# A two-layer trunk on one core: products of the output projection moved between the steps of the first attention's last head

## The chip, the core and the metric

The kernel runs on one core of one Trainium2 chip. The metric is the time of one execution on the device in microseconds. Before the change it is 2202.14 us, the median of 3 runs (2201.82 to 2206.84).

TensorE multiplies, VectorE, ScalarE and GpSimd work on tiles, SyncE issues the transfers. Each engine takes its instructions in order; semaphores order them between engines. SBUF is the on-chip memory, PSUM holds what TensorE writes.

## The reference

Sequence 1024, width 1024, two layers. The part that matters here is the first attention and its output projection:

```python
q = rms_norm(q, q_g) * (A_HEAD_DIM ** -0.5)      # 8 heads, 2 maps of 64 each
k = rms_norm(k, k_g)
...
logits = jnp.einsum('bqhcd,bkhcd->bhcqk', q_blk, k)
logits = logits - slopes * dist                  # chunk-causal mask
p = jax.nn.softmax(logits, axis=-1)
wts = p[:, :, 0] - lam * p[:, :, 1]
return jnp.einsum('bhqk,bkhe->bqhe', wts, v)     # per block of 128 queries
...
o = rms_norm(o, subln_g) * (1.0 - lambda_init)
return o.reshape(b, s, A_HEADS * A_V_DIM) @ w_o  # added to x
```

Behind it come a squared-ReLU MLP, shared keys and values, a second attention with a sliding window, and a second MLP.

## The kernel before, in words

Every operand of a matmul is a pair of a high part (a copy rounded by ScalarE) and a low part (the subtraction value minus high part), and a product is three matmuls: high x high, high x low, low x high. "High products" are the two that read the high part of the activations.

The attention works head by head; one head has eight steps, one for each block of 128 queries. In step s TensorE makes the scores of block s, VectorE adds the distances and takes the maxima (custom operation, L1730 or, in the last head, L1770) and their negation (`nm_a`), ScalarE the exponentials, and VectorE mixes the two maps: a reciprocal, a factor (`coef_a`, L1744) and the mixing itself (L1749, reads `p` and `p1`, writes `p`). TensorE transposes the mixed weights (L2233), ScalarE and VectorE make their high and low part (`wT_hi`, `wT_lo`), and TensorE multiplies them with the values into `pv`. In heads 0 to 6 the same steps carry the projection of the next head's queries, keys and values (`proj<-wa`), which fills TensorE. The last head (`last_head`) has none of it. Its order is written out by hand: ahead of the loop scores 0 and 1 and block 7 of head 6, then for s = 0 to 6 the transposes of block s, the scores of block s+2 and the values of block s.

Head outputs are normalised by GpSimd (`norm_steps` and one multiplication of 128x1024; for the last head VectorE does it), transposed and stored as chunk c of `oT`. ScalarE's `high_early(c)` copies chunk c into `a_hi`; VectorE subtracts it into `a_lo`.

The output projection has 8 panels of 128 output columns. A panel is 8 chunks x 2 halves of the sequence x 3 matmuls of 512 columns, 384 in all. Its weights come by DMA into `w_raw` (two buffers in `w_quad`) and are split into `w_hi`, `w_lo` (three slots in `w_op`, so panel 3 needs panel 0's slot). Before the change panels 0 and 1 are split in the last head. Behind the head's last values products TensorE makes the high products of chunks 0 to 6 for panels 0 and 1 (56), then the low ones (28), then in `segment` chunk 7 of both and all of panel 2, 3 and so on. `add_x(i)` on VectorE adds the residual stream (loaded into `quad`) to panel i and frees its bank; ScalarE then scales and squares it, and only then copies the high part of panel i+3 or, at i = 0, panel 3.

Of the kernel before, what the change touches and what calls it, by code (L numbers as in the profile page):

```python
# [32 lines left out]
ALU = mybir.AluOpType  # L33
ACT = mybir.ActivationFunctionType
F32 = mybir.dt.float32
# [4 lines left out]
P = 128  # L40
# [28 lines left out]
EARLY_LOW = 3  # L69
WB_AT = {1: (0, 1), 2: (1, 3), 3: (3, 4), 4: (4, 6), 5: (6, KC)}  # L70
# [96 lines left out]
def trunk(nc, io):  # L167
    ctx = ExitStack()
    with ctx:
# [58 lines left out]
        scope = ExitStack()  # L228
        x_tok = [sb("x_tok0", [P, 4, D], F32, scope)]
# [85 lines left out]
        w_quad = [sb(f"w_quad{i}", [P, 2, 4, 256], F32) for i in range(2)]  # L315
        w_op = sb("w_op", [P, 7, 2, HALF], F32R)
# [10 lines left out]
        def panel_parts(seg, i):  # L327

            return w_first if seg and i == 0 else (w_hi[i % 3], w_lo[i % 3])

# [20 lines left out]
        small_mm, sinks_done, lam_exp = sem("small_mm"), sem("sinks_done"), sem("lam_exp")  # L351
# [44 lines left out]
        out_tr, out_staged = sem("out_tr"), sem("out_staged")  # L396
        vs_in = sem("vs_in")


        dve_passed, act_passed = sem("dve_passed"), sem("act_passed")  # L400
# [194 lines left out]
        def _(sp):  # L595
# [49 lines left out]
            w_out = (io["a_w_o"][0], io["b_w_o"][0])  # L645
            w_up, w_down = io["mlp_w_up"], io["mlp_w_down"]

            def segment(seg):
# [3 lines left out]
                def load_wo(i):  # L652
                    if i >= 2 or seg:
                        sp.wait_ge(w_lo_done, KC * seg + i - 1)
                    sp.dma_start(w_raw[i % 2], wo[:, :, P * i:P * (i + 1)]).then_inc(w_in[i % 2], 16)
# [25 lines left out]
                load_wo(2)  # L681
                if seg == 0:
                    load_wo(3)
# [143 lines left out]
        def _(pool):  # L827
# [56 lines left out]
            run_heads(pool, head)  # L884

            def segment(seg):
# [12 lines left out]
                if seg == 0:  # L899
                    pool.wait_ge(tr_ready, 144)  # L900
                else:
                    pool.wait_ge(ot_free, 32)
                clear()
                def sum_weights(n, part):
# [130 lines left out]
        def _(act):  # L1035
# [23 lines left out]
            def first_head():  # L1059
# [19 lines left out]
                act.wait_ge(sinks_done, 1)  # L1079
# [4 lines left out]
                act.wait_ge(small_mm, 1)  # L1084
                nc.scalar.activation(lam_e[:, :], score[0][:, 0:2], ACT.Exp).then_inc(lam_exp, 1)
# [5 lines left out]
            def split_panel(panel):  # L1091
                i = panel % KC
                act.wait_ge(w_in[i % 2], panel // 2 * 16 + 16)
# [16 lines left out]
            def exps(h, s, par, i):  # L1110
                keys = P * (s + 1)
                act.wait_ge(nm_ready, h * NB + s + 1)
                act.sem_inc(act_passed, 1)
# [22 lines left out]
            def last_head():  # L1136
# [4 lines left out]
                def last_exps(s):  # L1141
                    keys, i = P * (s + 1), s % 2
                    act.sem_inc(act_passed, 1)
# [5 lines left out]

# [1612 lines left out]
```

## Time and profile before

| What | Value |
|---|---|
| median of the runs | 2202.14 us |
| profiled execution: span from first to last instruction | 2202.5 us |
| TensorE matmuls busy | 2147.4 us, 97% |
| VectorE | 1569.2 us, 71% |
| ScalarE | 1137.3 us, 52% |
| GpSimd | 758.0 us, 34% |
| mean granted clock of TensorE | 0.991 |

The page gives no time of the profiled execution beside its span. A line of a timeline is: start in us, duration in us, engine, line of the kernel, operation, output<-inputs, shape, count, and in brackets the idle time before it and what ended it. PE is TensorE, DVE VectorE, ACT ScalarE, POOL GpSimd. In merged lines (x7) the duration is that from the first start to the last end. Matmul ends are modelled, so the distance of two starts tells the rate. The granted clock is the share of 2.4 GHz that TensorE had; 0.5 is its lower level of 1.2 GHz.

### The profile page before, as it was taken

The page shows a single profiled execution, that of the slowest core. Times are in us where ns is not written, and L with a number is a line of the kernel's source. Part 1 is how long each engine was busy: PE and PEld are TensorE (multiplying, and loading weights), DVE is VectorE, ACT ScalarE, POOL GpSimd, SP SyncE. Part 2 cuts the span into 40 slices and gives each one's busy share as a digit, 9 for nine tenths or more (in the row PEclk, how much of TensorE's full clock was granted, in tenths as well). Part 3 has the DMA queues.
Part 4 walks back from the last instruction along what each step waited for, and adds up shares of the span by engine and source line. Part 5 has one row for each costly group of instructions (what it writes and reads, how often), then busy time and mean ns, then how long its engine had stood idle before and what let it go on. Part 6 is the DMA issues. An engine that isn't in the chain of part 4 may idle for free.

```text
span 2202.5 us, 34714 instructions
## 1 busy us (share of the span) xinstructions
PE 2147.4 (97%) x11580; PEld 1844.2 (84%) x11580; DVE 1569.2 (71%) x3012; ACT 1137.3 (52%) x2429; POOL 758.0 (34%) x1199
## 2 busy tenths in 40 slices
PE   7999999988999999999999999999999999999999
PEld 6999999977878888787888899988888888788787
DVE  6788788877586666778767757774766666886783
ACT  5566666655554555624434446764455555443342
POOL 2334333331642222333235225434622222322331
PEclk9999999999999999999999999999999999999999
DMA  6111110002424444754534121105244445754352
GB/s 201 47 30 30 29 29 22 1 20 96 131 99 158 157 146 142 273 178 171 191 124 160 63 55 48 29 19 164 91 158 156 141 141 212 259 191 144 104 183 85
DMA packets 190916, 257.71 MB, mean 117 GB/s; under 512 B 15136, under 2 KB 139552, under 8 KB 186144
## 3 DMA queue, kind: packets, MB, share of 16 engines
q1 hardware_dynamic: 190752, 255.65, 35.0%
q8 instruction: 87, 1.43, 0.3%
q14 instruction: 77, 0.63, 0.1%
HBM read 174.09 MB, written 79.69 MB: 115 GB/s over the span
## 4 chain that ended last, share of the span: by engine, by line
PE 80%; DVE 11%; issue 5%; ACT 2%; DMA 1%; POOLq 1%; DVEq 0%; POOL 0%; ACTq 0%; SPq 0%
PE score L2190 41%; PE proj L2190 15%; PE trb L2190 14%; PE pv L2190 6%; DVE xop L1543 4%; DVE w_op L1543 2%; DVE xT L1863 1%; PE trb L2233 1%; ACT p L1115 1%; DMA xop<-u_dram 1%; PE trb L2601 0%; PE trb L2287 0%; DVE p L1730 0%; PE trb L2261 0%; PE score L2588 0%
## 5 line engine op out<-in xcount | busy, mean ns | idle before, releaser
L2190 PE MATMUL score<-xop,w_op 128*128 128x512 f32 x3840 | 891.5, 391 | 7.2 <-DVE xT L1863 5.5
L2190 PEld LDWEIGHTS score<-xop,w_op 128*128 128x128 f32 x3840 | 722.3, 189 | 161.3 <-issue 11.0
L2190 PE MATMUL trb<-xop,w_op 128*128 128x512 f32 x1536 | 362.1, 391 | 5.4 <-DVE xT L1863 4.7
L897 POOL TENSOR_TENSOR w_quad<-w_quad,w_sum 128x512 f32<-128x512 f32 x64 | 83.8, 1309 | 777.0 <-DVE w_op L1543 777.0
L2190 PEld LDWEIGHTS trb<-xop,w_op 128*128 128x128 f32 x1536 | 287.3, 188 | 69.1 <-DVE w_op L1543 7.5
L1037 ACT ACTIVATE w_op<-w_quad 128x512 fp32r<-128x512 f32 (+1 forms) x336 | 213.9, 643 | 229.7 <-PE score L2190 106.6
L1543 DVE TENSOR_TENSOR w_op<-w_quad,w_op 128x512 fp32r<-128x512 f32 (+1 forms) x336 | 297.3, 890 | 40.8 <-ACT w_op L1037 40.7
L1863 DVE TENSOR_TENSOR xT<-score,xT 128x512 f32<-128x512 f32 x160 | 109.2, 686 | 138.0 <-PE score L2190 132.0
L1543 DVE TENSOR_TENSOR xop<-xop 128x1024 fp32r<-128x1024 f32 x112 | 150.6, 1361 | 3.5 <-ACT xop L1037 3.5
L1037 ACT ACTIVATE quad<-score 128x512 f32<-128x512 f32 x96 | 57.2, 596 | 176.0 <-PE score L2190 174.8
L1037 ACT ACTIVATE xop<-xop 128x1024 fp32r<-128x1024 f32 x112 | 117.0, 1053 | 56.5 <-DMA xop<-u_dram 56.2
L2190 PE MATMUL proj<-wa_hi,a_hi 128*128 128x384 f32 x418 | 142.5, 341 | 0.8 <-DVE v_parts L1544 0.8
L1115 ACT ACTIVATE p<-p,nm_a,slopes 128x128 f32<-128x128 f32 (+7 forms) x112 | 96.4, 862 | 90.4 <-DVE nm_a L1735 90.4
L2190 PE MATMUL proj<-wa_hi,a_lo 128*128 128x384 f32 x418 | 139.9, 335 | 0.0
L2190 PE MATMUL proj<-wa_lo,a_hi 128*128 128x384 f32 x418 | 139.8, 334 | 0.0
L1863 DVE TENSOR_TENSOR quad<-trb,quad 128x512 f32<-128x512 f32 x64 | 44.2, 690 | 106.0 <-PE trb L2190 72.2
L1037 ACT ACTIVATE w_op<-w_sum 128x512 fp32r<-128x512 f32 x128 | 76.9, 625 | 81.8 <-PE trb L2190 32.8
L2190 PE MATMUL score<-a_hi,w_op 128*128 128x512 f32 x368 | 112.8, 392 | 0.0
L519 POOL TENSOR_TENSOR chain_p<-rstd_qk 128x8 f32<-128x8 f32 x96 | 19.3, 201 | 248.8 <-DVE rstd_qk L511 239.5
L911 POOL TENSOR_TENSOR w_sum<-w_quad 128x512 f32<-128x512 f32 x64 | 90.0, 1407 | 36.2 <-DMA w_quad<-in_mlp_w_down 25.7
L897 POOL TENSOR_TENSOR w_quad<-w_quad 128x512 f32<-128x512 f32 x64 | 99.8, 1560 | 5.0
L1730 DVE CUSTOM_DVE_ANT_0 p<-score,dist_a 128x128 f32<-128x128 f32 (+7 forms) x112 | 80.3, 754 | 29.7 <-PE score L2190 29.7
(319 smaller groups left out, 4293.9 us busy)
## 6 DMA issues: line engine op xcount, KB each, us to landing
xop<-u_dram SPq DMA_DIRECT2D x112, 512.0 KB, 5.1
u_dram<-quad SPq DMA_DIRECT2D x32, 1536.0 KB, 9.7
w_quad<-in_mlp_w_up SPq DMA_DIRECT2D x64, 512.0 KB, 5.6
w_quad<-in_mlp_w_down SPq DMA_DIRECT2D x64, 512.0 KB, 4.9
wa_raw<-in_a_w_qkv SPq DMA_DIRECT2D x96, 128.0 KB, 2.4
quad<-xT_dram SPq DMA_DIRECT2D x32, 256.0 KB, 3.7
xT_dram<-xs SPq DMA_DIRECT2D x32, 256.0 KB, 2.4
u_dram<-quad SPq DMA_DIRECT2D x32, 256.0 KB, 3.8
```

Of the source, the lines that this page charges most:

```text
L519: eng.tensor_tensor(t, out, out, ALU.mult)
L897: return pool.tensor_tensor(out, x, y, ALU.subtract)
L911: pool.tensor_tensor(w_full(n, "S1"), quarter(n, 1, 0), quarter(n, 1, 1), ALU.add)\
L1037: return nc.scalar.activation(out, in_, ACT.Copy, scale=scale)
L1115: nc.scalar.activation(p[:, 0:keys], p[:, 0:keys], ACT.Exp, bias=nm_a[i][:, c:c + 1], scale=one(slopes, h), accum_out=ssum[par][:, c, s:s ...
L1543: return nc.vector.tensor_tensor(out, full, hi.bitcast(F32), ALU.subtract)
L1730: nc.vector.tensor_tensor_reduce(out=p[:, 0:keys], in0=score[c][:, 0:keys], in1=dist_a[:, S - keys:S], scale=1.0, scalar=LOWEST, op0=ALU.a ...
L1863: return nc.vector.tensor_tensor(out, a, b, ALU.add)
L2190: return nc.tensor.matmul(out, a, b, start=start, stop=stop, **kw)
L2233: last = nc.tensor.transpose(trb[b][:, P * (kc - 4 * i):P * (kc - 4 * i + 1)], p0[block_s % 2][:, P * kc:P * (kc + 1)], ident[:, :])
```

## The change

- Panel 2 is loaded into a place of its own and split in head 6 (step 2), first of all panels. Panel 0's high part is made at the beginning of the last head, panel 1's in its step 2; both low parts are GpSimd's.
- ScalarE makes the high parts of chunks 0 to 5 at the beginning of the last head; their low parts are GpSimd's, one behind the other, behind panel 1's.
- TensorE makes high products of chunks 0 to 5 of panel 2 between the steps of the last head, in the bank `proj`: first those of the right half (12). ScalarE copies the result into `kept`, and GpSimd adds it to the residual stream later, in `quad`. Then 12 of the left half. 12 more, of panel 1, stand ahead of the last values products.
- Behind the head stand the rest of chunks 0 to 5 for three panels, then chunk 6, then chunk 7; panel 2 is no longer a full panel in `segment`.
- Some semaphores are merged (`passed`, `lam_steps`), without a new wait.

```diff
+LATE = 6
+SPLIT_ORDER = (2, 0, 1, 3, 4, 5, 6, 7)
...
@@ sync: loads
+            sp.wait_ge(wa_lo_done, NH * 4)
+            sp.dma_start(w_raw2, w_out[0].rearrange("(k p) n -> p k n", p=P)[:, :, 2 * P:3 * P])\
+                .then_inc(w_in[0], 16)
...
@@ gpsimd
+                    if isinstance(h, int) and h == NH - 2 and s == NB - 1:
+                        low_panel()
...
+            def low_panel():
+
+                pool.wait_ge(w_lo_done, split_count(0, 2))
+                pool.wait_ge(w_hi_done, split_count(0, 0))
+                pool.tensor_tensor(w_lo[0], w_raw[0], w_hi[0].bitcast(F32), ALU.subtract).then_inc(w_lo_done, 1)
+
+            def last_head():
+
+                pool.wait_ge(o_rstd, NH - 1)
+                norm_steps(rstd_o[:, :], chain_o, NB)
...
+                pool.wait_ge(w_hi_done, split_count(0, 1))
+                pool.tensor_tensor(w_lo[1], w_raw[1], w_hi[1].bitcast(F32), ALU.subtract).then_inc(w_lo_done, 1)
+                for c in range(LATE):
+                    pool.wait_ge(o_early_hi, c + 1)
+                    pool.tensor_tensor(a_lo[:, c, :], oT[:, c, :], a_hi[:, c, :].bitcast(F32), ALU.subtract)\
+                        .then_inc(o_split, 1)
...
+                    x = quad[1][:, TILE[0, 1], :]
+                    pool.tensor_tensor(x, x, kept[0][:, :], ALU.add).then_inc(half_added, 1)
...
@@ scalar, last_head
+                high_early(0)
+                high_early(1)
                 last_exps(0)
                 high_wT(uses, 0)
+                split_panel(0)
+                high_early(2)
+                high_early(3)
...
                     if s == 1:
-                        high_early(0)
+                        high_early(4)
+                        high_early(5)
                     if s == 2:
+                        keep(0)
+                        split_panel(1)
                         high_pair(uses, h, 1, par)
...
-                    if s >= 4:
-                        high_early(s - 3)
...
-                    if s >= 5:
-                        split_panel(s - 5)
...
@@ vector
-                    if s == NB - 1:
-                        split_panel(0)
                     mix(h, s, par, s % 2)
...
-                split_panel(1)
...
-            for c in range(EARLY[0]):
+            dve.wait_ge(o_split, LATE)
+            for c in range(LATE, EARLY[0]):
...
@@ tensor
+            def panel_high(out, panel, half, chunks):
+
+                for c in chunks:
+                    pe.wait_ge(o_early_hi, c + 1)
+                    x_h = a_hi[:, c, HALF * half:HALF * (half + 1)]
+                    mm(out, w_hi[panel][:, c, :], x_h, c == 0, False)
+                    last = mm(out, w_lo[panel][:, c, :], x_h, False, c == LATE - 1 and (panel, half) == (2, 1))
+                return last
...
-                    for k in range(EARLY[seg] if i < 2 - seg else 0, KC):
+                    for k in range(EARLY[seg] if i < 3 - 2 * seg else 0, KC):
```

TensorE in the last head, step 5: transposes (`trb<-ident,p`), scores, values (`pv`). Before:

```order
L2233 MATMUL trb<-ident,p_1 128x128 [waits tr_free1]
L2233 MATMUL trb<-ident,p_1 128x128
L2190 MATMUL score<-kT_hi,qT_hi 128x512 [waits score_max]
...
L2190 MATMUL score<-kT_hi,qT_lo 128x512 x2
L2190 MATMUL pv<-v_parts,wT_hi 128x256 [waits tr_free1,tr_free0]
...
L2233 MATMUL trb<-ident,p_0 128x128 [waits tr_free0,mixed]
```

And after:

```order
L2247 MATMUL score<-kT_hi,qT_lo 128x512 x2
L2247 MATMUL proj<-a_hi,w_op 128x512 [waits o_early_hi]
L2247 MATMUL proj<-a_hi,w_op 128x512
...
L2247 MATMUL proj<-a_hi,w_op 128x512 [waits o_early_hi]
L2247 MATMUL proj<-a_hi,w_op 128x512
L2247 MATMUL pv<-v_parts,wT_hi 128x256 [waits tr_free1,tr_free0]
...
L2290 MATMUL trb<-ident,p_0 128x128 [waits tr_free0,mixed]
```

Six products of panel 2 now stand between the scores of block 7 and the values of block 5, ahead of the transposes of block 6.

GpSimd from the normalisation of head 6's output on. Before:

```order
L527 TENSOR_TENSOR rstd_o<-rstd_o,chain_p 128x8
L880 TENSOR_TENSOR xT<-xT,rstd_o 128x1024
L889 MEMSET ss 128x512 [waits tr_ready]
L889 MEMSET ss 128x512
L897 TENSOR_TENSOR quad<-quad 128x512 [waits h_ready]
```

And after:

```order
L542 TENSOR_TENSOR rstd_o<-rstd_o,chain_p 128x8
L915 TENSOR_TENSOR xT<-xT,rstd_o 128x1024
L918 TENSOR_TENSOR w_op<-w_quad,w_op 128x1024 [waits w_hi_done]
L921 TENSOR_TENSOR a_lo<-xT,a_hi 128x1024 [waits o_early_hi] x6
L929 MEMSET ss 128x512 [waits tr_ready,half_kept]
L929 MEMSET ss 128x512
L948 TENSOR_TENSOR quad<-quad,kept 128x512 [waits quad_in1]
L937 TENSOR_TENSOR quad<-quad 128x512 [waits h_ready]
```

Seven subtractions of 128x1024 stand where GpSimd had nothing until the end of the head.

TensorE in `segment`, from chunk 7 of panel 2 (`proj` and `pv`) to panel 3 (`score`). After the change:

```order
L2247 MATMUL proj<-a_hi,w_op 128x512 [waits o_split,w_lo_done]
L2247 MATMUL proj<-a_lo,w_op 128x512
L2247 MATMUL proj<-a_hi,w_op 128x512
L2247 MATMUL pv<-a_hi,w_op 128x512
L2247 MATMUL pv<-a_lo,w_op 128x512
L2247 MATMUL pv<-a_hi,w_op 128x512
L2247 MATMUL score<-a_hi,w_op 128x512 [waits o_split,xs_ready,w_lo_done]
```

Panel 2 has 6 products left there; before it had all its 48 between panel 1 and panel 3.

## Rows read from the trace of the kernel before

**Rows 1.** Windows: length, PE, PEld, DVE, ACT, POOL busy us (count), clock, DMA

```profile
460.00:480.00 20.00, 17.57 (x124) 16.01 (x123) 15.76 (x46) 10.47 (x24) 5.33 (x19) 0.97 0.20 53
480.00:500.00 20.00, 15.10 (x89) 11.47 (x90) 16.71 (x53) 13.45 (x37) 8.24 (x24) 0.78 0.01 1
500.00:520.00 20.00, 13.85 (x85) 11.81 (x82) 17.20 (x33) 17.39 (x37) 0.00 (x0) 0.82 0.18 51
620.00:640.00 20.00, 18.70 (x84) 14.22 (x84) 18.56 (x27) 9.26 (x18) 12.03 (x9) 1.00 0.21 65
640.00:660.00 20.00, 20.00 (x90) 16.53 (x89) 13.70 (x22) 11.30 (x21) 6.35 (x5) 1.00 0.43 146
```

**Rows 2.** Waits of TensorE, 470 to 700 us

```profile
PE pv L2190 <- DVE wT_lo L1543: 7.1, 4, 2.2
PE score L2190 <- DVE mx_a L1770: 4.1, 4, 1.5
PE trb L2233 <- DVE p L1749: 1.3, 2, 0.9
```

**Rows 3.** Timeline of VectorE, mixings of steps 4, 5 and 6

```profile
496.57 0.89 DVE L1749 SCALAR_TENSOR_TENSOR p<-p,coef_a,p 128x640 f32<-128x640 f32 x1
...
501.76 1.02 DVE L1749 SCALAR_TENSOR_TENSOR p<-p_last,coef_a,p 128x768 f32<-128x768 f32 x1
...
507.19 1.15 DVE L1749 SCALAR_TENSOR_TENSOR p<-p,coef_a,p 128x896 f32<-128x896 f32 x1
```

**Rows 4.** Timeline of TensorE in the last head

```profile
477.63 0.36 PE L2190 MATMUL pv<-v_parts,wT_hi 128*128 128x256 f32 x1 [2.14 <-DVE wT_lo L1543]
...
509.78 0.93 PE L2233 MATMUL trb<-ident,p 128*128 128x128 f32 x7
...
519.40 0.37 PE L2190 MATMUL pv<-v_parts,wT_hi 128*128 128x256 f32 x1 [2.22 <-DVE wT_lo L1543]
...
522.77 9.41 PE L2190 MATMUL score<-a_hi,w_op 128*128 128x512 f32 x40
```

**Rows 5.** Timeline of TensorE, first products of panels 2 and 3

```profile
545.59 0.39 PE L2190 MATMUL proj<-a_hi,w_op 128*128 128x512 f32 x1
...
556.47 0.39 PE L2190 MATMUL score<-a_hi,w_op 128*128 128x512 f32 x1
```

**Rows 6.** Timelines of ScalarE and VectorE: weights' copy; splits of panels 3 and 5

```profile
475.59 1.06 ACT L1037 ACTIVATE wT_hi<-trb 128x512 fp32r<-128x512 f32 x2
...
546.83 1.04 ACT L1037 ACTIVATE w_op<-w_quad 128x1024 fp32r<-128x1024 f32 x1
...
547.91 1.69 DVE L1543 TENSOR_TENSOR w_op<-w_quad,w_op 128x1024 fp32r<-128x1024 f32 x1 [2.78 <-ACT w_op L1037]
...
567.61 1.21 DVE L1543 TENSOR_TENSOR w_op<-w_quad,w_op 128x1024 fp32r<-128x1024 f32 x1
```

**Rows 7.** Timelines of VectorE and GpSimd in earlier heads

```profile
129.89 0.22 DVE L1744 SCALAR_TENSOR_TENSOR coef_a<-ssum,neg_lam,rcp_a 128x1 f32<-128x1 f32 x1
...
134.00 1.08 DVE L1744 SCALAR_TENSOR_TENSOR coef_a<-ssum,neg_lam,rcp_a 128x1 f32<-128x1 f32 x1
134.02 1.05 POOL L873 TENSOR_TENSOR qk<-qk,rstd_qk 128x512 f32<-128x512 f32 x1
...
385.38 1.90 POOL L880 TENSOR_TENSOR xT<-xT,rstd_o 128x1024 f32<-128x1024 f32 x1
...
385.53 1.77 DVE L1735 TENSOR_SCALAR nm_a<-mx_a,slopes 128x2 f32<-128x2 f32 x1
```

**Rows 8.** Timelines of GpSimd and VectorE, last head and behind it

```profile
490.92 2.34 POOL L880 TENSOR_TENSOR xT<-xT,rstd_o 128x1024 f32<-128x1024 f32 x1
...
491.42 0.82 DVE L1770 CUSTOM_DVE_ANT_0 p<-score,dist_a 128x640 f32<-128x640 f32 x1
...
599.29 1.30 POOL L897 TENSOR_TENSOR w_quad<-w_quad 128x512 f32<-128x512 f32 x1
...
614.52 1.28 DVE L1543 TENSOR_TENSOR xop<-quad,xop 128x512 fp32r<-128x512 f32 x2
...
619.74 3.46 DVE L1543 TENSOR_TENSOR xop<-quad,xop 128x512 fp32r<-128x512 f32 x2
```

More of the change, by code:

```diff
@@ L228, in trunk @@
         scope = ExitStack()
+        kept = [sb(f"kept{i}", [P, HALF], F32, scope) for i in range(1)]
+        scope.close()
+        scope = ExitStack()
         x_tok = [sb("x_tok0", [P, 4, D], F32, scope)]
@@ L329, in panel_parts, with split_count @@
             return w_first if seg and i == 0 else (w_hi[i % 3], w_lo[i % 3])
+        def split_count(seg, panel):
+            return KC * seg + (panel if seg else SPLIT_ORDER.index(panel)) + 1
         oT = xT
@@ L680, in segment @@
                 load_wo(1)
-                load_wo(2)
-                if seg == 0:
-                    load_wo(3)
+                load_wo(2 if seg else 3)
                 sp.wait_ge(o_split, KC * seg + 5)
@@ L1092, in split_panel @@
                 i = panel % KC
-                act.wait_ge(w_in[i % 2], panel // 2 * 16 + 16)
+                act.wait_ge(w_in[i % 2], panel // 2 * 16 + (16 if panel else 32))
                 if i >= 3 or panel == KC + 2:
@@ L1225, in head @@
                         wa_split(h + 2, par == 0, 0, 1)
+                    if s == 2 and isinstance(h, int) and h == NH - 2:
+                        act.wait_ge(w_in[0], 16)
+                        copy(w_hi[2], w_raw2).then_inc(w_hi_done, 1)
                     if s == O_STEP and tail:
@@ L1699, in head @@
                         low_pair(uses, h, s, par)
+                    if s == 2 and isinstance(h, int) and h == NH - 2:
+                        dve.wait_ge(w_hi_done, split_count(0, 2))
+                        low(w_lo[2], w_raw2, w_hi[2]).then_inc(w_lo_done, 1)
                     if s in (2 if attn else 4, NB - 1) and more:
@@ L1882, in add_x @@
                         dve.wait_ge(quad_in[u % 2], 64 * (2 * seg + u // 2 + 1))
+                        if seg == 0 and (i, half) == (2, 1):
+                            dve.wait_ge(half_added, 1)
                         if i:
@@ L2362, in head, with panel_low @@
                         values(uses, s, (s - 1) % NB, h * 4 + (s - 1) // 2, par if s else 1 - par)
+            def panel_high(out, panel, half, chunks):
[5 more added lines that the diff above has]
+                return last
+            def panel_low(out, panel, half, chunks, first):
+                for c in chunks:
+                    pe.wait_ge(o_split, c + 1)
+                    mm(out, w_hi[panel][:, c, :], a_lo[:, c, HALF * half:HALF * (half + 1)], first and c == 0, False)
             def panel_products(seg, panel, x_hi, x_lo, k):
@@ L2396, in _ @@
             transpose_weights(last_uses, 0, NB - 1, NH * NB - 1)
+            pe.wait_ge(score_max, 2 * NH * NB)
+            pe.wait_ge(w_lo_done, split_count(0, 1))
+            panel_high(wo_bank[0][1][0], 1, 0, range(LATE))
             values(last_uses, 0, NB - 1, NH * 4 - 1, 1)
[L2400 to L2415 removed]
+            panel_high(wo_bank[0][1][1], 1, 1, range(LATE))
+            for half in range(2):
+                panel_high(wo_bank[0][0][half], 0, half, range(LATE))
+            transpose_outputs(last_uses, NH, 1)
+            for half in range(2):
+                panel_low(wo_bank[0][0][half], 0, half, range(LATE), False)
+            for half in range(2):
+                panel_low(wo_bank[0][1][half], 1, half, range(LATE), False)
+            pe.wait_ge(pv_free, NH * 4)
+            for half in range(2):
+                panel_low(wo_bank[0][2][half], 2, half, range(LATE), half == 1)
+            for panel in range(3):
+                for half in range(2):
+                    panel_high(wo_bank[0][panel][half], panel, half, range(LATE, EARLY[0]))
+            for panel in range(3):
+                for half in range(2):
+                    panel_low(wo_bank[0][panel][half], panel, half, range(LATE, EARLY[0]), False)
             def segment(seg):
                 for i in range(KC):
[L2419 removed]
+                    pe.wait_ge(w_lo_done, split_count(seg, i))
                     if i >= 3:
```

97 lines of the change are left out of this document (56 added, 41 removed).

## The prediction

> **What bounds the kernel now.** I read the windows of 20 us first [rows 1]. TensorE is busy in all of a window after the first attention (640 to 660 us: 20.00 of 20), but only 17.57, 15.10 and 13.85 us in the three windows from 460 to 520 us. That is the last head of the first attention, which ends at 522.77 us [rows 4]. In two of them the granted clock is 0.78 and 0.82. So everywhere else TensorE sets the time, and here something else does. The list of waits [rows 2] names it: 7.1 us for the low parts of the transposed weights, 4.1 us for the maxima, 1.3 us for the mixed weights, all by VectorE. VectorE's own line in that head is serial: mixing of step s, two maxima of step s+1, two exponentials on ScalarE, mixing of step s+1. The mixings start at 496.57, 501.76 and 507.19 us [rows 3], 5.2 and 5.4 us apart, and VectorE has 17.20 us of work in 20 [rows 1]. A delay of one mixing therefore moves the end of the head by nearly as much; work given to TensorE's gaps does not, as long as it fits.
>
> The clock shows in the matmuls. The sixteen values products of the last block, 256 columns each, stand between 519.40 and 522.77, behind a gap of 2.22 us: 0.211 us each, which is the 1.2 GHz level [rows 4]. From 522.77 on TensorE runs without a gap and at full clock: 48 products of 512 columns lie from 545.59 to 556.47, 0.227 us each [rows 5].
>
> **What the change removes.** The output panels have the same 384 products. Before, all of them stand behind 522.77. Now 24 lie between the head's steps and 12 ahead of the last values products, so 348 remain: 36 x 0.227 = 8.2 us less behind the last head. That is the whole direct gain. The gaps that ought to take the 36 are there: rows 2 sum to 12.5 us, with 2.14 us where four of them go and 2.22 us where twelve go. VectorE also loses the low parts of two panels in the head and of six chunks and a panel behind it, but none is on the line: the first ran beside the last exponentials, and TensorE did not wait for any of those behind. ScalarE has less to do at the very end, worth at most the 1.0 us of one such copy. The early split of panel 2 in head 6 (one ScalarE copy of 1.04 us, one VectorE subtraction of 1.2 us, both [rows 6]) lies in a stretch in which TensorE is full and VectorE is not: nothing, with 1.2 us as the price if it is not covered.
>
> **What it adds: GpSimd beside VectorE.** Eight subtractions of 128x1024 go to GpSimd: the low part of panel 0 at the beginning of the head, that of panel 1 and of six chunks in its second half. The trace before has none of this size. One of 128x512 with two tensors takes 1.30 us and the next starts behind it; the normalisation of 128x1024 takes 1.90 us [rows 7, 8]. I take 2.4 us each, from 1.9 to 2.6.
>
> Rows 7 show what such an operation does to VectorE. The negated maxima took 1.77 us, started 0.15 us into a GpSimd operation of 1.90 us and until its end; the mixing's factor, 0.22 us elsewhere, took 1.08 us against a GpSimd operation of 1.05 us. Where GpSimd has one operation behind the other, it takes the turn after each of VectorE's: two subtractions with two SBUF tensors take 1.28 us alone and 3.46 us beside it, 1.73 each [rows 8]. The maxima, which read PSUM and one SBUF tensor, are not hit: 0.82 us in the middle of GpSimd's normalisation, 491.42 against 490.92 [rows 8]. Of the chain, the factor and the mixing have two tensors in SBUF. The Trainium skill ("SBUF — State Buffer", section "SBUF: two separate sides") has a rule that speaks against this change: the port pair of VectorE and GpSimd is an exclusive lock, and the loser blocks for the whole instruction. By that rule each collision costs the rest of a GpSimd operation; were bandwidth merely shared, a mixing of 1 us could lose about 1 us. The trace agrees with the lock.
>
> Now the line, step by step. *Step 0.* ScalarE finishes the copies of the last weights of head 6 at 476.65 [rows 6], then panel 0's high part, 477.6. GpSimd's first subtraction runs from 477.7 to 480.1; the factor of mixing 0, ready at 478.7, waits: +1.5 to 2.1 us, of which waits that were there before take some. I keep +1.3 us. *Step 4.* GpSimd's normalisation ended at 493.26 before (490.92 + 2.34, rows 8), now about 494.5. Panel 1: to 497.0. Chunk 0: to 499.4. The factor, due 0.3 us ahead of mixing 4 and 1.3 to 1.9 us later than before (497.6 to 498.2), waits to 499.4; chunk 1 takes the turn between factor and mixing, to 502.0. Mixing 4 starts at 502.0, not 496.57: +5.4. *Step 5.* Due 5.2 us later. Chunks 2 and 3 run 502.9 to 507.7, the factor follows, chunk 4 goes ahead of the mixing: 510.3, not 501.76: +8.5. *Step 6.* Chunk 5 is over at 513.7 and the factor is due at 515: no wait, +8.1. Bounds for this item: 2 mixings x 2.4 = 4.8 us if all the factors fall free, 9.5 if none does; and, if VectorE were served first each time, 2 us.
>
> *Steps 6 and 7 on TensorE.* Six products now stand between the last scores and the values of block 5, ahead of the transposes of block 6, which start at 509.78 [rows 4], 1.4 us behind the mixing's end, and which ScalarE's last exponentials follow. At full clock they cost 1.4, at half 2.6 us. Delayed as above TensorE has long gaps, so I expect much of it at the lower level: +1.6, from 0 to 3.1. *The end.* Twelve products, 2.7 to 5.1 us, go into a gap of 2.2: +1 to 2; against that the last values products may get the full clock (3.4 us down to half of it) and ScalarE is free earlier: +0.4, from -1.5 to +1.5. The head ends 8.1 + 1.6 + 0.4 = 10.1 us later.
>
> **What it adds behind.** Before, panel 2's 48 products (545.59 to 556.47) covered the preparation of panel 3, whose slot is free only when panel 0 is complete: ScalarE's copy at 546.83 to 547.87, VectorE's subtraction at 547.91 to 549.60 [rows 6]. Panel 0 completes at 544.2 in that time. Now panels 1 and 2 have 12 products left after it, 2.7 us, so TensorE is there at 546.9 and waits until 549.6: 2.7 us. No other engine gets sooner there; ScalarE has the scaled and squared chunk 0 in front. The gap of 2.22 us in rows 4 was followed by 3.4 us at the lower level, which cost half of that: I take 1.3, from 0 to 1.7. From panel 4 on VectorE is ready in time, at its times of before: panel 5's subtraction ends at 568.8 [rows 6], and TensorE, at 549.6 + 1.3 + 2 x 10.9, asks for it at 572.7. The 1.3 us TensorE lacks at 620 to 640 [rows 1] is a wait that moves with panel 7. The copy of the half panel (0.6 us, ScalarE) and its addition (1.3 us, GpSimd) lie in idle time, as the early loads do.
>
> **Sum.** -8.2 + 10.1 + 2.7 + 1.3 = +5.9 us on the profiled span of 2202.5 us, which is 0.4 above the median of 2202.14. The page gives no other time for that execution. Forecast: 2202.1 + 5.9 = 2208.0 us; the case's own range is 2203 to 2213.
>
> **Rivals.** (A) *The gaps win.* VectorE is hit once a step or less, the head ends only 2 us later or not at all. For it: no mixing in the trace was ever longer than its shape asks, even with GpSimd starting right behind. Against it: the factor in front always took the wait, and GpSimd had nothing more queued. -8.2 + 2 + 4 = -2.2 us, 2200; without the 2 us and with the last values products at full clock, -6, 2196. If panel 3's low part were ready as well, -10: the case spans 2192 to 2202. The Trainium skill ("TensorE: Matmul & The Clock Gate", part 1) says that activity releases the clock; by it, filled gaps would speed up the last values products and more in the head; the rows show only that gaps above 2 us came before the lower level. (B) *The clock falls with the longer head.* Place: steps 5 to 7. With 9 us steps TensorE is idle nearly half of each, and scores, six products and values all run at 1.2 GHz: +3.1 in place of 1.6, twelve products 5.1, values 3.4, chain +9.5. Sum +10: 2212 us. It decides from the point at which GpSimd's operations cost more than about 8 us. (C) *The 24 products are not hidden.* TensorE was late for the transposes of block 6 even before (1.4 us, above); then the head only grows by what is moved into it, with GpSimd harmless: -8.2 + 8 + 4 = +4, 2206 us.
>
> **Chances.** Forecast 0.52, A 0.24, B 0.14, C 0.10. About 0.3% (6.6 us: 2195.5 and 2208.7) is what a measurement of this kernel tells from no change. Slower by more: under half of the forecast's case (0.23), most of B (0.13), a little of C (0.02): 0.38. Faster by more: under half of A, 0.10. Within: 0.52. Range 2196 to 2213: it holds the forecast's case, C, the lower half of B and over half of A.
>
> **What would show it.** In the profile after: mixings of 640 and 768 elements starting 2 us or more behind their factor; a factor of 1 us and more; mixing 6 near 515; the last values products ending near 532; a wait of 2.7 us of TensorE for a low part, with all panels behind complete. If the mixings keep a distance of 5.2 us, the second term is wrong and A holds. If TensorE runs through from panel 2 to 3, the third is.

## The result, and the profile after

| | median | ratio to the kernel before |
|---|---|---|
| kernel before | 2202.86 us (17 runs) | |
| kernel after | 2209.04 us (17 runs) | 1.0024, interval 1.0018 to 1.0030 |

The change makes the kernel 0.24% slower, some 5.3 us, with 36 products taken out from behind the last head. The forecast was 2208.0 us. The profiled execution after has a span of 2207.7 us, clock 0.992.

To compare traces I measure from a common point, the start of the mixing of 128x1024 in head 6: 471.80 us before, 473.20 after. In the fourteen traces of this study it lies between 468.2 and 473.2, and the changed kernel itself has it at 473.20 and, in run 5, at 472.28. Of the 1.4 us between the two, 1.1 us are there at TensorE's first product already (8.1 and 9.2 us); 0.1 us is head 6, in which the change splits panel 2. Each row is one trace. Distances to the starts of the named operations, in us ("MLP" is the one behind the first attention):

| | mixing 4 | 5 | 6 | 7 | last values product | first MLP product | end of span |
|---|---|---|---|---|---|---|---|
| before | 24.8 | 30.0 | 35.4 | 42.6 | 50.8 | 139.1 | 1730.7 |
| after | 27.5 | 35.0 | 42.5 | 49.6 | 56.4 | 140.6 | 1734.5 |

Windows of 20 us, columns as in rows 1 with GB/s at the end, after:

```profile
480.00:500.00 20.00, 14.55 (x93) 11.41 (x93) 16.59 (x54) 14.32 (x35) 14.93 (x31) 0.91 0.03 7
500.00:520.00 20.00, 14.39 (x81) 11.24 (x79) 18.74 (x32) 9.70 (x25) 13.50 (x6) 0.83 0.23 73
520.00:540.00 20.00, 17.80 (x101) 15.38 (x101) 9.64 (x25) 6.99 (x18) 0.89 (x2) 1.00 0.00 1
540.00:560.00 20.00, 17.67 (x74) 14.27 (x73) 5.28 (x6) 6.16 (x9) 6.09 (x5) 0.95 0.55 176
...
600.00:620.00 20.00, 19.14 (x84) 15.21 (x82) 13.75 (x14) 10.08 (x18) 16.43 (x12) 1.00 0.30 97
```

GpSimd is busy for 14.93 and 13.50 us where it had 8.24 and 0.00 [rows 1]. TensorE lacks 2.3 us at 540 to 560 and 0.9 at 600 to 620, where it was busy for 20.00 of 20 before:

```profile
540.00:560.00 20.00, 20.00 (x90) 16.57 (x89) 7.80 (x8) 9.62 (x16) 11.73 (x8) 1.00 0.75 242
...
600.00:620.00 20.00, 20.00 (x89) 16.44 (x88) 15.74 (x18) 14.27 (x27) 13.10 (x10) 1.00 0.32 106
```

VectorE's factors and mixings of steps 4 to 6, and beside them GpSimd, after:

```profile
499.59 1.01 DVE L1801 SCALAR_TENSOR_TENSOR coef_a<-ssum,neg_lam,rcp_a 128x1 f32<-128x1 f32 x1
500.68 2.89 DVE L1806 SCALAR_TENSOR_TENSOR p<-p,coef_a,p 128x640 f32<-128x640 f32 x1
...
507.83 0.34 DVE L1801 SCALAR_TENSOR_TENSOR coef_a<-ssum,neg_lam,rcp_a 128x1 f32<-128x1 f32 x1
508.24 3.04 DVE L1806 SCALAR_TENSOR_TENSOR p<-p_last,coef_a,p 128x768 f32<-128x768 f32 x1
...
515.69 1.15 DVE L1806 SCALAR_TENSOR_TENSOR p<-p,coef_a,p 128x896 f32<-128x896 f32 x1
```

```profile
495.88 2.38 POOL L918 TENSOR_TENSOR w_op<-w_quad,w_op 128x1024 fp32r<-128x1024 f32 x1
498.21 15.29 POOL L921 TENSOR_TENSOR a_lo<-xT,a_hi 128x1024 fp32r<-128x1024 f32 x6
```

Mixing 4 takes 2.89 us for 0.89 of work, mixing 5 3.04 for 1.02 [rows 3]. Each lost 2.0 us inside its own row, so the wait stands in the duration and not as a distance from the factor. GpSimd waits in the same way: of the six subtractions in the merged row, four take 2.34 to 2.40 us, and the two during which a mixing had its turn take 2.94 and 3.10. The third mixing, behind GpSimd's end at 513.5, has its old 1.15 us. TensorE at the head's end, at panel 3 and at the MLP's operands, after:

```profile
525.00 3.01 PE L2247 MATMUL score<-a_hi,w_op 128*128 128x512 f32 x12
527.85 0.28 PE L2247 MATMUL pv<-v_parts,wT_hi 128*128 128x256 f32 x1
...
557.66 0.50 PE L2247 MATMUL score<-a_hi,w_op 128*128 128x512 f32 x1 [2.33 <-DVE w_op L1597]
...
613.80 2.61 PE L2247 MATMUL score<-xop,w_op 128*128 128x512 f32 x9
617.15 0.96 PE L2247 MATMUL score<-xop,w_op 128*128 128x512 f32 x3 [0.74 <-DVE xop L1597]
```

Sixteen values products now lie between 527.85 and 529.76: 0.12 us each, the upper clock level, against 0.211 in rows 4. The wait of 2.33 us at panel 3 is new. So is one of 0.74 us for an operand of the MLP.

### The profile page after: what moved, and what is told of

It reads as the page before. It is cut to its first block, busy times and chain, and to the rows that moved or that the text cites. A ratio compares the mean times of both kernels' runs of the same rounds, so it can differ in the third digit from the quotient of the medians.

```text
span 2207.7 us, 34721 instructions
## 1 busy us (share of the span) xinstructions
PE 2146.4 (97%) x11580; PEld 1840.8 (83%) x11580; DVE 1571.0 (71%) x3004; ACT 1138.0 (52%) x2430; POOL 781.1 (35%) x1208
## 4 chain that ended last, share of the span: by engine, by line
PE 76%; DVE 12%; issue 6%; ACT 2%; POOL 2%; DMA 1%; POOLq 1%; DVEq 0%; SPq 0%; ACTq 0%
PE score L2247 39%; PE proj L2247 15%; PE trb L2247 13%; PE pv L2247 6%; DVE xop L1597 4%; DVE w_op L1597 2%; DVE xT L1918 1%; PE trb L2290 1%; ACT p L1161 1%; POOL quad L937 1%; DMA xop<-u_dram 1%; POOL ss L934 1%; PE trb L2693 1%; PE trb L2344 0%; DVE p L1787 0%
## 5 line engine op out<-in xcount | busy, mean ns | idle before, releaser
L1787 DVE CUSTOM_DVE_ANT_0 p<-score,dist_a 128x128 f32<-128x128 f32 (+7 forms) x112 | 80.3, 754 | 27.2 <-PE score L2247 27.1
```

Source lines behind the costliest of these rows:

```text
L1787: nc.vector.tensor_tensor_reduce(out=p[:, 0:keys], in0=score[c][:, 0:keys], in1=dist_a[:, S - keys:S], scale=1.0, scalar=LOWEST, op0=ALU.a ...
```

## The experiments

Twelve runs in three groups (1 to 4, 5 to 8, 9 to 12), each group against the kernel before on the same chip (medians 2201.83, 2201.95 and 2201.66 us, so times of different groups are compared by their ratios). The intervals are 0.09 to 0.14% wide to each side, 2 to 3 us; a smaller difference between two runs is read from the traces, one for each run, or stays open. Distances as above:

| | ratio (interval) | mixing 4 | 5 | 6 | 7 | last values | first MLP | end |
|---|---|---|---|---|---|---|---|---|
| 1 chunks' low parts to VectorE | 1.0019 (1.0009 to 1.0028) | 25.6 | 30.9 | 36.4 | 43.5 | 50.3 | 137.6 | 1730.9 |
| 2 before + GpSimd work | 1.0038 (1.0024 to 1.0052) | 27.2 | 35.2 | 41.4 | 48.6 | 55.0 | 143.1 | 1734.8 |
| 3 GpSimd behind the mixings | 0.9988 (0.9979 to 0.9997) | 23.5 | 28.9 | 34.3 | 41.4 | 48.2 | 130.7 | 1726.9 |
| 4 panel 3 first | 1.0021 (1.0011 to 1.0030) | 28.5 | 36.1 | 43.6 | 50.6 | 57.5 | 137.5 | 1733.2 |
| 5 changed, again | 1.0021 (1.0010 to 1.0031) | 27.5 | 35.0 | 42.5 | 49.6 | 56.4 | 140.7 | 1734.6 |
| 6 panel 0 first | 1.0007 (0.9999 to 1.0016) | 27.5 | 35.0 | 42.5 | 49.6 | 56.4 | 136.3 | 1730.4 |
| 7 runs 3 and 6 | 0.9974 (0.9965 to 0.9983) | 24.8 | 29.9 | 35.4 | 42.5 | 49.3 | 129.2 | 1723.3 |
| 8 twelve behind | 1.0034 (1.0021 to 1.0047) | 27.5 | 35.0 | 42.5 | 49.7 | 56.6 | 143.6 | 1735.9 |
| 9 run 6, addition later | 1.0009 (1.0000 to 1.0018) | 28.5 | 36.1 | 43.5 | 50.6 | 57.4 | 137.4 | 1728.8 |
| 10 run 7, addition later | 0.9972 (0.9961 to 0.9982) | 24.8 | 30.0 | 35.4 | 42.5 | 49.3 | 129.3 | 1722.6 |
| 11 run 10, load later | 0.9966 (0.9954 to 0.9979) | 23.5 | 28.8 | 34.3 | 41.4 | 48.2 | 128.2 | 1720.8 |
| 12 values first | 1.0042 (1.0028 to 1.0056) | 28.2 | 35.7 | 43.2 | 51.8 | 59.3 | 147.9 | 1740.9 |

### GpSimd beside the mixings: runs 1, 2 and 3

Run 1 takes GpSimd's chunks away:

```diff
-                for c in range(LATE):
-                    pool.wait_ge(o_early_hi, c + 1)
-                    pool.tensor_tensor(a_lo[:, c, :], ...).then_inc(o_split, 1)
...
-            dve.wait_ge(o_split, LATE)
-            for c in range(LATE, EARLY[0]):
+            for c in range(EARLY[0]):
```

> The changed kernel with the six low parts of the activations given back to VectorE, behind the last head; the two low parts of weights stay with GpSimd. Theory (GpSimd's long two-input operations block the factor and then the mixing): only panel 1's subtraction is left beside the mixings, so mixing 4 starts near 498.6 instead of 500.7, mixing 5 near 503.8 instead of 508.2, mixing 6 near 509 instead of 515.7; the last values products end about 6 us earlier (523 to 524). Behind the head VectorE makes seven low parts at 1.15 us each and is late for TensorE by 1 to 3 us. Median 2203.5 to 2207 against 2209.0 of the changed kernel. Rival (the six products between steps and the longer TensorE path set the head's length, GpSimd is harmless): the head ends where it did, 529 to 530, and the time is 2210 or more.

The mixings are back within 1.0 us of before, and the head ends 6.1 us earlier than after the change (50.3 against 56.4), with all 36 products where the change put them. TensorE waited three times 0.63 us for VectorE's chunks, 1.9 us in all. Little of it reaches the end: 2205.54 us, by the ratio 1 us under the changed kernel, which the intervals don't separate, and 3.6 us by the trace. The chunks cost 1.9 us of waits, and the granted clock behind these was 0.57 and 0.58 from 536 to 540 us, an estimated 1.7 us more. Waits of 2.5 us at panel 3 and 2.2 us at the MLP's operands followed. So a head of the old length alone doesn't make this kernel faster than the kernel before: the low parts that GpSimd had made in the head are missed behind it.

Run 2 adds GpSimd's work alone to the kernel before:

```diff
+            def last_head():
+                head(NH - 1, 1, True, True, False, False)
+                ...
+                for c in range(7):
+                    last = pool.tensor_tensor(a_lo[:, c, :], w_raw[1], w_raw[1], ALU.subtract)
```

> The kernel before with one addition: GpSimd makes seven more subtractions of 128x1024 behind its normalisation in the last head, into a place that is free there (their result is overwritten unread). Nothing else is changed, TensorE's work least of all. Theory (lock, and GpSimd takes the turn between factor and mixing): mixing 4 starts near 500.5 instead of 496.57, mixing 5 near 508.5 instead of 501.76, mixing 6 near 514 instead of 507.19; the last values products end 6 to 7.5 us later; median 2208.5 to 2210.5 against 2202.9. Rival one (a lock, but VectorE is served next): only the factor waits, 1 to 2 us in all, head 2 to 3.5 us longer, 2205 to 2206.5. Rival two (shared bandwidth or no contention; the lengthening in the changed kernel comes from TensorE's products): less than 1.5 us, 2203 to 2204.5.

2209.16 us, 0.38% slower. Without a single product moved, this is at least as slow as the changed kernel. The profiled execution was the fastest of the five, 2204.79 us; its trace shows 4.1 us of the 8 (1734.8 against 1730.7), and where the rest arises in the slower executions it can't show. One line was added on VectorE too, a wait for the last subtraction ahead of the split of panel 1; that subtraction ends at 503.3 us, well ahead of it. VectorE and GpSimd there:

```profile
493.49 1.86 DVE L1752 SCALAR_TENSOR_TENSOR coef_a<-ssum,neg_lam,rcp_a 128x1 f32<-128x1 f32 x1
495.42 2.44 DVE L1757 SCALAR_TENSOR_TENSOR p<-p,coef_a,p 128x640 f32<-128x640 f32 x1
501.72 1.62 DVE L1752 SCALAR_TENSOR_TENSOR coef_a<-ssum,neg_lam,rcp_a 128x1 f32<-128x1 f32 x1
503.41 1.02 DVE L1757 SCALAR_TENSOR_TENSOR p<-p_last,coef_a,p 128x768 f32<-128x768 f32 x1
```

```profile
489.74 13.58 POOL L889 TENSOR_TENSOR a_lo<-w_quad 128x1024 fp32r<-128x1024 f32 x7
```

A factor of one column took 1.86 and 1.62 us instead of 0.22, and the mixing behind the first took 2.44 instead of 0.89: GpSimd took the turn between the two. Taken singly, its third subtraction ends at 495.33, where the factor ends (495.35), and its fourth runs from 495.30 to 497.18, inside the mixing. Mixings 4, 5 and 6 came 2.4, 5.2 and 6.0 us later, where 3.9, 6.7 and 6.8 were expected; these subtractions, whose two operands are one tile, took 1.89 us each when undisturbed, not 2.4. Rival two falls. Rival one too, by the second row: had VectorE been served next, that mixing would have kept its 0.89 us.

Run 3 leaves GpSimd five of the eight subtractions and releases each by a mixing's end (`ON_POOL` is 3; VectorE makes the other chunks behind the head):

```diff
+                pool.wait_ge(mixed, (NH - 1) * NB + 4)
+                low_panel()
+                pool.wait_ge(mixed, (NH - 1) * NB + 5)
                 pool.wait_ge(w_hi_done, split_count(0, 1))
...
-                for c in range(LATE):
+                for c in range(ON_POOL):
+                    pool.wait_ge(mixed, (NH - 1) * NB + 6 + min(c, 1))
```

> The changed kernel with GpSimd's subtractions each released by the end of a mixing: panel 0 behind mixing 3, panel 1 behind mixing 4, chunk 0 behind mixing 5, chunks 1 and 2 behind mixing 6; chunks 3 to 6 by VectorE behind the head. Theory (lock): each subtraction of 2.4 us fits between a mixing and the next factor (some 4 us), so mixings 4, 5 and 6 start within 0.7 us of their times before the change (496.6, 501.8, 507.2); the last values products end at 523 to 524.5 instead of 529.8; median 2202 to 2204.5 against 2209.0. Rival (sharing: what GpSimd does costs VectorE the same wherever it stands): the head still ends 4 us or more later than before the change, 2206 or more.

2197.53 us, 0.12% faster than before the change and by the ratios 8 us under the changed kernel. The five subtractions that stay in GpSimd lengthen none of VectorE's factors and mixings when they stand behind a mixing:

```profile
498.43 2.38 POOL L924 TENSOR_TENSOR a_lo<-xT,a_hi 128x1024 fp32r<-128x1024 f32 x1 [3.11 <-DVE p L1809]
504.00 4.73 POOL L924 TENSOR_TENSOR a_lo<-xT,a_hi 128x1024 fp32r<-128x1024 f32 x2 [3.19 <-DVE p L1809]
```

```profile
497.34 1.02 DVE L1809 SCALAR_TENSOR_TENSOR p<-p_last,coef_a,p 128x768 f32<-128x768 f32 x1
502.47 0.22 DVE L1804 SCALAR_TENSOR_TENSOR coef_a<-ssum,neg_lam,rcp_a 128x1 f32<-128x1 f32 x1
502.76 1.15 DVE L1809 SCALAR_TENSOR_TENSOR p<-p,coef_a,p 128x896 f32<-128x896 f32 x1
```

Between the mixings at 497.34 and 502.76 VectorE's maxima read PSUM; GpSimd's 2.38 us fit beside them, and the factor keeps 0.22 us. The head ends 2.6 us earlier than before the change, with the 36 products in it: 520.0 on the scale of the trace before, 3 us better than the 523 to 524.5 expected. I had counted the products at the end as a cost. Some 1.1 us of the 2.6 go with the clock of this one execution: it was 1.00 all through the head, while runs 7 and 10, with the same head and 0.88 to 0.95 from 480 to 500 us, have mixing 4 at 24.8 and the end at 49.3. The time too is below what was expected: by the ratio 2200.2 us on the scale of 2202.86, against 2202 to 2204.5. The Trainium skill ("SBUF — State Buffer", section "SBUF: two separate sides") calls the port pair of the two engines an exclusive lock; by that rule the waits of runs 2 and 3 come out as they did, and both traces agree.

### TensorE's products in the head: runs 5, 8 and 12

Run 5 is the changed kernel again. Run 8 takes twelve products of steps 4 to 6 back behind the head. Run 12 does so with the twelve of panel 1:

```diff
-                    if s == 4: ... panel_high(proj[:, :], 2, 0, (0,))
-                    if s == 5: ... (1, 2, 3)
-                    if s == 6: ... (4, 5)
...
             panel_high(wo_bank[0][1][1], 1, 1, range(LATE))
+            pe.wait_ge(half_kept, 1)
+            panel_high(proj[:, :], 2, 0, range(LATE))
```

```diff
-            panel_high(wo_bank[0][1][0], 1, 0, range(LATE))
             values(last_uses, 0, NB - 1, NH * 4 - 1, 1)
+            panel_high(wo_bank[0][1][0], 1, 0, range(LATE))
```

> The changed kernel once more, unaltered, to stand beside the other runs of this chip: 1.0024 times the kernel before, that is 5 to 6 us above it.

> The changed kernel with the twelve products of panel 2's left half taken out of steps 4, 5 and 6 of the last head and put behind its last values products; the rest as changed. Prediction's term (six products in steps 6 and 7 lengthen the head by 1.6 us): the head ends 1.6 us earlier, 12 x 0.227 = 2.7 us come behind it, median 1.1 us above the changed kernel. Theory now, from the trace (with mixings held up by GpSimd the twelve products lie wholly in TensorE's gaps): the head ends where it did, median 2.2 to 3 us above the changed kernel. Rival (the head's own length follows TensorE's work): no more than the changed kernel.

> The changed kernel with the twelve products of panel 1 moved from ahead of the last values products to behind them. Prediction's term (twelve products against the clock of the values, in all +0.4 us for the head): the head ends 0.4 us earlier, 2.7 us more behind it, +2.3 us. Theory from the trace (the twelve keep TensorE busy so that the sixteen values products run at 0.12 us each and not 0.21, and they fill what is otherwise a wait): without them TensorE waits about 2.2 us for the low part of the weights, the values take 3.4 us, and the head ends at the same time or up to 0.6 us later; the time is 2.5 to 3.5 us above the changed kernel. Rival (the values run at full clock anyway): the head ends 1 us earlier or more, the time is 1.7 us above or less.

Run 8: the last values product at 56.6 against 56.4, the first MLP product 2.9 us later, the median 2.3 us above run 5, as expected (the intervals overlap; the 2.9 us of the trace carry the reading). The twelve had been hidden; the head's length does not follow them. Run 12: the values of the last block and what is ahead of them:

```profile
512.69 0.64 PE L2247 MATMUL score<-kT_hi,qT_lo 64*128 64x512 f32 x2
513.26 2.10 PE L2247 MATMUL proj<-a_hi,w_op 128*128 128x512 f32 x6
...
516.62 0.93 PE L2290 MATMUL trb<-ident,p 128*128 128x128 f32 x7
...
525.34 0.55 PE L2247 MATMUL pv<-v_parts,wT_hi 128*128 128x256 f32 x1 [1.67 <-DVE wT_lo L1597]
525.69 0.41 PE L2247 MATMUL pv<-v_parts,wT_lo 128*128 128x256 f32 x1
525.90 0.41 PE L2247 MATMUL pv<-v_parts,wT_hi 128*128 128x256 f32 x1
```

The values go at 0.21 us each (525.69 to 525.90), the lower level, behind a gap of 1.67 us. From mixing 7 to the last values product it is 7.4 us; 6.8 with the twelve in front. The time is about 4 us above the changed kernel by the ratios, more than the 2.5 to 3.5 expected, and the head ends 2.9 us later (59.3 against 56.4), where 0.6 at most was expected. In the trace 2.2 of the 2.9 us lie ahead of mixing 7, on which this edit has no hold: in this execution the scores of block 7 (510.57 to 513.3) also ran at the lower level, and the transposes of block 6 began at 516.62, 2.9 us behind their mixing's end (1.4 us after the change), so mixing 7 came 8.6 us behind mixing 6. It is 7.1 in the traces of runs 4, 5, 6 and 9. This is the prediction's term for steps 6 and 7, at its price, in one execution of the six that carry those products beside GpSimd's chunks.

### Behind the head: runs 4, 6, 7, 9, 10 and 11

Run 4 moves ScalarE's copy of panel 3 ahead of the scaled chunk 0:

```diff
                 for i in range(KC - 1):
+                    if i == 0 and not seg:
+                        split_panel(3)
-                    if i + 2 < KC and (seg or i):
+                    if i + 2 < KC and (seg or i > 1):
                         split_panel(KC * seg + i + 2)
```

> The changed kernel with one line's order changed on ScalarE: the copy of panel 3's high part stands ahead of the scaled and squared chunk 0, not behind. Theory (panel 3's low part is late because its preparation starts only when panel 0 is complete, and the wait of 2.3 us brings the lower clock): the copy runs about 2.4 us earlier, TensorE waits 0.5 us or less at panel 3, no product behind it is at the lower level, and what is behind comes 3 to 4 us earlier: median 2205 to 2206.5 against 2209.0. Rival (the wait only moves: the chunk 0 work that is now later delays the residual panel 3 or GpSimd's sums, and the MLP starts as late): 2207.5 to 2209.

The wait at panel 3 is gone. By the ratio the time is that of run 5, 1.0021. Waits of TensorE from 596 to 660 us (total, times, longest):

```profile
PE score L2249 <- DVE xop L1599: 3.4, 2, 2.6
PE proj L2249 <- DVE ss L1978: 0.3, 1, 0.3
```

What TensorE gained at panel 3 it waited for at the MLP's first operands, 3.4 us, with the clock from 600 to 620 us at 0.91. The wait moved, as the rival had it; something else is due there. Whether all of the time went with it stays open: from the last values product to the end the trace has 2.3 us less than the changed kernel, and the ratios don't resolve that.

Run 6 changes only the order of TensorE's products, so that panel 0 is complete first and the others' products stand behind it:

```diff
             transpose_outputs(last_uses, NH, 1)
-            ... low products, chunk 6 and its low part, panel by panel
...
+                    if seg == 0 and i < 3:
+                        ... the same for panel i, just ahead of its chunk 7
                     for k in range(EARLY[seg] if i < 3 - 2 * seg else 0, KC):
```

> The changed kernel with TensorE's order behind the last head altered: after the high products and the transposes panel 0 is brought to its end first (low products, chunk 6, chunk 7), then panel 1, then panel 2. Not one product more or less. Theory (from the completion of panel 0 a chain of VectorE, ScalarE and GpSimd runs to the first MLP product, some 62 us long; in the changed kernel only 57 us of products stand behind that completion, so the excess is waited for, first at panel 3 and the rest at the MLP's start): panel 0 is complete about 7.5 us earlier, no wait at panel 3 and none at the MLP's start, no product there at the lower clock: median 4.5 to 6 us under the changed kernel, 1.0000 to 1.0005 of the kernel before. Rival (only panel 3's wait and its clock go, the loss at the MLP's start comes from GpSimd's later sums and stays): 3 to 4 us under the changed kernel. Rival two (chunk 7 isn't ready that early, TensorE waits for it instead): 2 us or less.

Run 7 is that order in the kernel of run 3.

> The kernel with GpSimd's subtractions released by the mixings, and with panel 0 brought to its end first. If the two losses are separate and add: the run with the released subtractions had 2.3 us of wait at panel 3, 2.3 us at the MLP's start and stretches at the lower clock behind both; without them 5 to 6.5 us less than that run: ratio to the kernel before 0.9955 to 0.9965, near 2192 us. If the head's gain hid them or the chain only moves the wait to chunk 7's low part: 0.9975 or more.

Run 6 is some 3 us under run 5: panel 3's wait and its lower clock are gone, and the MLP's wait grew to 2.3 us. So the first rival held (3 to 4 us, against the 4.5 to 6 of my theory), and my chain of 62 us from panel 0 is no constant. Panel 0's sum stood at 540.30 in run 6, 70.5 us behind the common point, against 78.8 after the change, and the MLP's first product came only 4.3 us earlier. GpSimd shows what came between (run 6):

```profile
535.61 1.00 POOL L929 MEMSET ss<- 128x512 f32 x2 [25.57 <-PE trb L2318]
549.17 1.29 POOL L948 TENSOR_TENSOR quad<-quad,kept 128x512 f32<-128x512 f32 x1 [12.56 <-DMA quad<-xT_dram]
550.42 1.29 POOL L937 TENSOR_TENSOR quad<-quad 128x512 f32<-128x512 f32 x1
```

The addition of the kept half stands at the head of GpSimd's queue and waits 12.56 us for a transfer. Behind it stand the sums of chunk 0, scaled since 542.4. ScalarE waited for GpSimd in turn (0.9 and 0.6 us, squares of panel 1). VectorE has a wait of its own there: its sum for panel 1 starts at 549.96, after 4.28 us for the transfer that parks panel 0. Runs 9 and 10 put the addition behind the sums; run 11 also moves a load of 1 MB that went out ahead of these transfers:

```diff
-                    x = quad[1][:, TILE[0, 1], :]
-                    pool.tensor_tensor(x, x, kept[0][:, :], ALU.add).then_inc(half_added, 1)
...
                             add_square(square_of(c, half), half, 36 * seg + 2 * c + half + 1)
+                    if seg == 0 and c == 0:
+                        ... the same wait and addition
```

```diff
                 sp.wait_ge(o_split, KC * (seg + 1))
-                load_pair(0)
+                if seg:
+                    load_pair(0)
                 load_unit(1)
...
+                    if i == 1 and seg == 0:
+                        load_pair(0)
```

> As the run with panel 0 brought to its end first, and GpSimd's addition of the kept half panel is moved behind its sums of panel 0 (before, it stands ahead of them and waits for the DMA of the second unit of the residual stream). Theory: that wait in GpSimd's queue (until 549.2 us there, 8 us behind the scaled chunk 0) holds up the squares of panel 1 and through them the whole row of sums and splits; without it GpSimd's first sum starts within 2 us of the scaled chunk 0, and TensorE's wait for the MLP's first operand goes from 2.3 us to 0.3 or less: 2 to 3 us under the run without this move, 0.9990 to 1.0000 of the kernel before. Rival (VectorE's own row of splits sets the MLP's start, whatever GpSimd does): the wait of 2.3 us stays, the time is the same within 0.7 us.

> The same move of the addition in the kernel that also has GpSimd's subtractions released by the mixings. By the theory its waits for the MLP's operands (1.5 us) go: 1 to 2.5 us under the run without the move, 0.9962 to 0.9970 of the kernel before, near 2194 us. By the rival no change from 0.9974.

> As the run before this one, and the load of the MLP's first weights (1 MB) goes out behind the parking of panel 1 and no longer ahead of the residual's second unit. If the DMAs set the pace of VectorE's panel 1 (it waited 4.3 us for the parked panel 0), VectorE's second sum starts 2 us or more earlier and the waits at the MLP's start are gone for good: 0.5 to 2 us less. If GpSimd alone was the cause: no difference (within 0.7 us).

In run 9 GpSimd's first sum starts at 542.80, beside the scaled chunk, and TensorE's wait for MLP operands falls from 2.3 to 0.7 us; in run 10 from 1.5 to 0.7. VectorE's wait for the parked panel stays in both (3.70 and 3.59 us). In run 11 both waits are 0, and VectorE's second sum starts at 537.20, 68.4 us behind the common point (73.0 in run 10). The ratios can't tell: 1.0007 to 1.0009, 0.9974 to 0.9972, then 0.9966. From the last values product to the end the traces have 2.7 us less in run 9 than in run 6, and 0.7 less at each of the steps from run 7 to 10 and to 11. So the waits are seen to go, and their worth in time is not settled. Run 7 (0.9974 for 0.9955 to 0.9965), run 9 (1.0009 for 0.9990 to 1.0000) and run 10 (0.9972 for 0.9962 to 0.9970) all gained less than I expected: the two losses don't simply add. Run 11 is the best kernel, 2193.30 us: 0.34% faster than the kernel before, with no overlap of its interval with 1.

## Why the prediction came out, step by step

- *The 36 products, -8.2.* Held. From the last values product to panel 3's start it was 33.9 us [rows 5] and is 28.0: -5.9, which is -8.2 and the wait of 2.33. To the first MLP product it was 88.3 us and is 84.2: -4.1, with the clock's term below.
- *Step 0, +1.3.* Mixings 1 to 3 are 1.2 us later from the common point. What waited for GpSimd was not the factor but a 128x4 operation ahead of it (last section).
- *Mixings 4 to 6, +5.4, +8.5, +8.1.* The order of turns was as worked out. With the 2.0 us that stand inside the rows, the real starts are 29.5, 37.1 and 42.5: +4.7, +7.1, +7.1. Each is 0.7 to 1.4 us less. Runs 1 to 3 show that GpSimd's place alone does it.
- *TensorE in steps 6 and 7, +1.6.* Mis-sized here. The transposes of block 6 start 1.4 us behind the mixing, as before; TensorE ran at the upper level from 510.4 us on. Run 12 shows the other case, 1.5 us. So this term hangs on the granted clock of block 7's scores and the six products, and its case was the exception, one trace of six.
- *The end, +0.4.* From mixing 7 to the last values product 6.8 us instead of 8.1: -1.3, near the -1.5 that stood as the bound. Run 12 takes it apart: without the twelve products the values start 4.1 us behind the mixing (5.0 before the change, when ScalarE and VectorE still had panels to split there) and need 3.3 us; with them they start at 5.0 and need 1.8. Of the predicted 10.1 us of the head these two terms missed 3.4 and the mixings 1.0: it is 5.7.
- *Panel 3's low part, +2.7, and the clock behind it, +1.3.* 2.33 us, and from panel 3's start to the first MLP product 56.14 us instead of 54.40 [rows 5], with no wait in between and the clock at 0.96 from 560 to 580: +1.7.
- *Costed at nothing.* The early split of panel 2 cost 0.1 us. "The addition lies in idle time" was wrong as an argument: with a transfer to wait for it holds up what stands behind it in GpSimd's queue, by 8 us in run 6. In the changed kernel itself it is less: the addition starts at 554.01 and the first sum at 555.26, 1.8 us behind its operand, and no run moves it there alone, so its share in the time after the change is not shown. And the slack of the MLP's start, which I let move with panel 7, was used up: runs 1, 3, 4 and 6 show 2.2 to 3.4 us there as soon as TensorE comes earlier. From the first MLP product to the end it is 2.3 us more than before. The wait of 0.74 us is part of that; the rest is open.

Sum from the common point: +5.7 - 4.1 + 2.3 = +3.9 (3.8 by the table), and 1.4 us ahead of it. Forecast +5.9, measured +5.3 by the ratio. The mechanism was right: GpSimd beside the mixings and the wait at panel 3 eat up what the 36 products give. That the numbers agree so closely is partly luck: the head was 4.4 us too long in the forecast, 2.3 us behind were not in it, and the profiled execution began late.

Of the rivals, A's condition was wrong. Its price is met by run 3, which keeps GpSimd away from the factor and the mixing (0.9988, 2200 on its scale), but not by run 1, where the head is as short and the kernel is at 1.0019: A left out that somebody must make the low parts in time. B did not occur as a whole. C is refuted by run 8 for the twelve products that it moves, and by run 2, in which GpSimd is not harmless.

## What to carry to other kernels

Before moving two-input SBUF work to GpSimd, list VectorE's operations with two SBUF operands on the critical line, and release each GpSimd operation right behind one of them, where it has time to end before the next; in run 3 no factor and no mixing was longer for it. Filling the gaps of one stage shortens the cover of the next: count what stands behind the first result on which the splits wait, and finish that result first. An operation in "idle time" needs its waits read as well as its duration.

## What the runs showed of the hardware that was not expected

- Some of VectorE's smallest operations wait for GpSimd's whole instruction too: 2.32 us for one of 128x4 after the change (the same instruction takes 0.23 at 472.04), and a factor of one column 1.86 us in run 2. Others don't: the negated maximum of a single column took no more than 0.22 us in any trace, with two to nine of them starting inside a long GpSimd operation in each.

```profile
479.13 2.40 POOL L908 TENSOR_TENSOR w_op<-w_quad,w_op 128x1024 fp32r<-128x1024 f32 x1 [9.21 <-ACT w_op L1083]
```

```profile
479.24 2.32 DVE L1771 TENSOR_SCALAR chain_q<-stat_m,msq 128x4 f32<-128x4 f32 x1
```

- A subtraction of 128x1024 on GpSimd took 2.34 to 2.40 us with two sources and 1.89 us when both operands were the same tile (run 2). One that a mixing met took 0.6 to 0.7 us more: each of the two engines waits for the other.
- Short gaps can come before the lower clock level: in run 1 three of 0.63 us between 532 and 535 us did, with the clock at 0.57 from 536 to 538.
- The clock level inside the head differs from one execution to the next of nearly the same program, and moves the head by 1 to 2.5 us: in the five traces with the whole changed head (after, runs 4, 5, 6 and 9) mixing 4 stands at 27.5 to 28.5 and the last values product at 56.4 to 57.5. In run 12, which had the lower level near 480 to 483 us and again at 512 to 514, mixing 7 is at 51.8 instead of 49.6 to 50.6.
